# Routing of eight heads in batches, with pair sums only where they can be among the best 16

## The reference, cut to what matters

```python
def block(xb):
    qry = (xb @ wq).reshape(PEER_BLOCK, R_HEADS, 2, HALF_KEY)
    s = jnp.einsum('prsk,snk->prsn', qry, subkeys)
    s1, i1 = lax.top_k(s[:, :, 0], PEER_TOPK)       # 16 of 128
    s2, i2 = lax.top_k(s[:, :, 1], PEER_TOPK)
    cand_s = (s1[..., :, None] + s2[..., None, :]).reshape(..., 256)
    cand_i = (i1[..., :, None] * N_KEYS + i2[..., None, :]).reshape(..., 256)
    top_s, top_pos = lax.top_k(cand_s, PEER_TOPK)   # 16 of 256
    idx = jnp.take_along_axis(cand_i, top_pos, axis=-1)
    gate = jax.nn.softmax(top_s, axis=-1)
    u = jnp.take(u_tab, idx, axis=0)
    act = jax.nn.gelu(jnp.einsum('prkd,pd->prk', u, xb))
    v = jnp.take(v_tab, idx, axis=0)
    return jnp.einsum('prk,prkd->pd', gate * act, v)
```

## Time and profile before

| what | us |
|---|---|
| median of three runs | 6728.52 (6718.85 to 6743.54) |
| the profiled execution | 6727.06 |
| its span, first to last instruction | 6725.2 |
| DVE busy in the span | 4249.0 |
| POOL busy in the span | 3074.3 |
| expert part of the first layer, first dot to last sum | 1867.1 |

### The profile page before, as it was taken

The page is one execution under the profiler, slowest core; times in us unless marked ns, Lnnn a source line. Parts: engine busy times, 40 slices in busy tenths (PEclk is TensorE's granted clock), DMA queues, the critical chain, the costliest instruction groups (busy, mean ns, idle before and its releaser), DMA issues. The chain is left out here.

```text
span 6725.2 us, 54716 instructions
## 1 busy us (share of the span) xinstructions
PE 4633.8 (69%) x17681; PEld 2732.2 (41%) x17681; DVE 4249.0 (63%) x8313; ACT 1205.2 (18%) x2414; POOL 3074.3 (46%) x2828
## 2 busy tenths in 40 slices
PE   7989886998665627170889898869986655362617
PEld 3785555564222202020347855565642222120202
DVE  2551448049788798988325514571597887979783
ACT  2421143010111101010124211430101111010101
POOL 0000012027777777777600000120277777777775
PEclk8999988999887869595979999989998888686959
DMA  4001010659999999999930011006599999999998
GB/s 144 26 0 38 25 38 3 232 206 344 375 344 355 373 412 372 409 377 409 361 114 25 0 39 37 25 21 229 216 340 387 334 376 371 409 369 407 367 413 331
DMA packets 506080, 1623.44 MB, mean 241 GB/s; under 512 B 48148, under 2 KB 60586, under 8 KB 505658
## 3 DMA queue, kind: packets, MB, share of 16 engines
q0 software_dynamic: 368640, 1342.34, 51.7%
q1 hardware_dynamic: 137202, 278.23, 11.4%
HBM read 1601.45 MB, written 21.56 MB: 241 GB/s over the span
## 5 line engine op out<-in xcount | busy, mean ns | idle before, releaser
L1167 PE MATMUL ps<-slab,arena 128*128 128x512 f32 x744 | 356.1, 616 | 674.1 <-DMA slab<-in_peer_v,peer_idxs 670.6
L1167 PE MATMUL ps<-arena 128*128 128x512 f32 x1128 | 528.6, 604 | 84.1 <-DMA arena<-in_peer_v,peer_idxs 70.0
L731 PE MATMUL ps<-hT,slab 128*128 128x512 f32 (+1 forms) x2048 | 568.5, 439 | 6.1 <-DVE arena L1687 6.1
L1167 PE MATMUL ps<-states,arena 128*128 128x512 f32 x792 | 378.9, 620 | 264.4 <-DMA states<-in_peer_v,peer_idxs 230.3
L2273 POOL DMA_INDIRECT arena<-in_peer_u,peer_idxs x400 | 478.1, 1195 | 176.9 <-issue 98.6
L1525 ACT ACTIVATE arena<-consts,arena 128x128 f32<-128x128 f32 x800 | 313.7, 400 | 1264.0 <-PE ps L1167 1259.7
L2120 DVE CUSTOM_DVE_ANT_0 arena<-arena 128x1024 f32<-128x1024 f32 x400 | 494.2, 1242 | 34.0 <-DMA arena<-in_peer_u,peer_idxs 30.5
L1167 PEld LDWEIGHTS ps<-slab,arena 128*128 128x128 f32 x744 | 135.0, 193 | 891.3 <-DMA slab<-in_peer_v,peer_idxs 660.5
L2273 POOL DMA_INDIRECT states<-in_peer_u,peer_idxs x300 | 359.1, 1197 | 266.9 <-PE ps L1123 149.0
L2273 POOL DMA_INDIRECT arena<-in_peer_v,peer_idxs x400 | 420.4, 1051 | 132.7 <-issue 94.0
L1167 PE MATMUL ps<-hT,arena 128*128 128x512 f32 x456 | 219.6, 619 | 375.1 <-DMA hT<-in_peer_v,peer_idxs 371.3
(11 more groups left out here) (323 smaller groups left out, 9370.2 us busy)
## 6 DMA issues: line engine op xcount, KB each, us to landing
slab<-in_w_in SPq DMA_DIRECT2D x50, 2048.0 KB, 7.8
slab<-in_ada_w SPq DMA_DIRECT2D x18, 2048.0 KB, 8.4
arena<-in_w_branch SPq DMA_DIRECT2D x24, 1024.0 KB, 12.2
slab<-in_w_out SPq DMA_DIRECT2D x8, 2048.0 KB, 12.3
arena<-mod_scratch SPq DMA_DIRECT2D x28, 512.0 KB, 9.0
arena<-in_ada_w SPq DMA_DIRECT2D x6, 2048.0 KB, 9.8
slab<-in_peer_wq SPq DMA_DIRECT2D x6, 2048.0 KB, 19.6
x_scratch<-arena SPq DMA_DIRECT2D x16, 512.0 KB, 5.5
```

The source lines that it names most:

```text
L731: last = mm(bank(i0 + c, part), wt[:, k, c * P:(c + 1) * P], hT[:, k, t0:t0 + tn], start=(k == 0), stop=(k == KC - 1))
L1167: last = mm(ps[4 + half][:, :], diag[i % DIAGS], row(e, 1, j)[:, 512 * half:512 * half + 512], start=(i == 0), stop=(j == PE_SLOTS[-1]))
```

## The change

Two things are changed in routing. First, heads are routed in batches: in block 0 heads 0 and 1, then 2 to 4, then 5 to 7; in the other blocks four and four. All that follows the passes over the scores is done for the batch in one operation. Second, the table of pair sums shrinks from 256 to 54 columns. In two falling lists the pair (i, j) cannot be among the best 16 when (i + 1)(j + 1) > 16; five rectangles (`RECTS`) cover what is left. A place in the 54 columns is turned into i and j without shift and mask: the places at which rows i begin (`starts`) are compared with it, and the differences of neighbouring first numbers, summed up to i, give the first key's number; the place minus the row's start gives j.

Part of the diff:

```diff
+RECTS = ((0, 0, 1, 16), (16, 1, 2, 8), (24, 2, 4, 5), (34, 4, 8, 3), (46, 8, 16, 1))
+N_CAND = 54
+BATCH = 4
...
-                cand3 = PK["cand"].rearrange("p (i j) -> p i j", j=TOPK)
...
-                    elif step < 24:
-                        side = (step - 18) // 3
-                        pos, out = (("pi", "e1"), ("pj", "e2"))[side]
-                        if (step - 18) % 3 == 0:
-                            w(dk, "e1" if side else "pj")
-                            dk.mark(tt(cand3, bc_last(PK[pos], TOPK), bc_mid(C["iota"], TOPK), ALU.is_equal), ("eq", side))
-                        elif (step - 18) % 3 == 1:
-                            w(dk, ("eq", side))
-                            dk.mark(tt(cand3, cand3, bc_mid(PK["tif"][:, TOPK * side:TOPK * side + TOPK], TOPK), ALU.mult), ("eqv", side))
-                        else:
-                            w(dk, ("eqv", side))
-                            dk.mark(v.tensor_reduce(PK[out], cand3, AX.X, ALU.add), out)
...
+                def routing(e, first, last, spare):
...
+                    for i in range(nr):
                         if e == 0:
+                            dve.wait_ge(scored, first + i + 1)
+                        for side in (0, 1):
+                            c, o = 256 * (first + i) + P * side, 32 * i + TOPK * side
+                            yield from top16(dk, tv[:, o:o + TOPK], ti[:, o:o + TOPK], PK["sc"][:, c:c + P], (i, side))
...
+                    for c0, i0, i1, n in RECTS:
+                        rows_, shape = i1 - i0, [P, nr, i1 - i0, n]
+                        dk.mark(tt(cand3[:, :, c0:c0 + rows_ * n].rearrange("p r (i j) -> p r i j", j=n),
+                                   tv3[:, :, i0:i1].unsqueeze(3).broadcast_to(shape),
+                                   tv3[:, :, TOPK:TOPK + n].unsqueeze(2).broadcast_to(shape), ALU.add), ("cand", c0))
+                        yield
+                    w(dk, ("cand", RECTS[-1][0]))
+                    for i in range(nr):
+                        o = TOPK * i
+                        yield from top16(dk, fv[:, o:o + TOPK], fp[:, o:o + TOPK], cand[:, N_CAND * i:N_CAND * (i + 1)], ("c", i))
...
+                    dk.mark(tt(tv3[:, :, 1:TOPK], ti3[:, :, 1:TOPK], ti3[:, :, 0:TOPK - 1], ALU.subtract), "d1")
+                    yield
+                    shape = [P, nr, TOPK, TOPK]
+                    reached = PK["sc"][:, 256 * first:256 * last]
...
+                    dk.mark(tt(flat(reached), bc_last(fpf, TOPK), bc_mid(C["starts"], TOPK * nr), ALU.is_ge), "reached")
+                    yield
...
+                    dk.mark(tt(flat(spare), flat(reached), bc_mid(C["dstarts"], TOPK * nr), ALU.mult), "start_parts")
+                    yield
...
+                    dk.mark(v.tensor_reduce(pj, flat(spare), AX.X, ALU.add), "start")
+                    yield
...
+                    dk.mark(tt(four(reached), four(reached), tv3[:, :, 0:TOPK].unsqueeze(2).broadcast_to(shape), ALU.mult), "e1_parts")
+                    yield
...
+                    dve.sem_clear(dk.sem)
+                    dve.sem_inc(routed, nr)
...
-                dots(0, routing(0, 2, R_HEADS), lambda j: 2, (100, 122, 124, 126))
+                def rest_of_first_block():
+                    for first in (2, 5):
+                        yield from routing(0, first, first + 3, ACC_ALL[:, 0:768])
+                dots(0, rest_of_first_block(), lambda j: 3, (100, 122, 124, 126))
```

More of the change, by code:

```diff
@@ L60, in _layout @@
                     ("posq1", P), ("posk0", 1), ("posk1", 1), ("rot", P), ("cos", TS), ("sin", TS),
[L61 removed]
+                    ("iota", TOPK), ("starts", TOPK), ("dstarts", TOPK), ("eps5", 1), ("eps6", 1), ("sel", GROUPS * P)):
         CONST_COLS[name] = (at, n)
@@ L83, in constants @@
     row = lambda v: np.broadcast_to(v, (P, len(v)))
+    starts = np.concatenate([at + n * np.arange(i1 - i0) for at, i0, i1, n in RECTS])
     value = {
@@ L90, in constants @@
         "posk0": P - 1 - j, "posk1": j, "rot": rot, "cos": np.cos(ang), "sin": np.sin(ang),
-        "iota": row(np.arange(TOPK)), "eps5": np.full((P, 1), LN_EPS), "eps6": np.full((P, 1), NORM_EPS),
+        "iota": row(np.arange(TOPK)), "starts": row(starts), "dstarts": row(np.diff(starts, prepend=0)), "eps5": np.full((P, 1), LN_EPS), "eps6": np.full((P, 1), NORM_EPS),
         "sel": (j == np.arange(GROUPS * P)[None, :] // P),
@@ L290, in trunk_program @@
         ex = [Stage(f"ex{e}", csem, plan) for e in range(NB)]
-        route = Stage("route", csem, plan, "dve")
-        STAGES = ([mods1, dnp, dn, dno, rtp, rt, rto, hgp, hg, hgo, mods2] + [st[g] for st in (merge, resid, peq) for g in GRP] + ex
-                  + [route])
+        route_sem = csem("route")
+        route = {n: Marks(route_sem, plan, ("route", n)) for n in (2, 3, 4)}
+        STAGES = ([mods1, dnp, dn, dno, rtp, rt, rto, hgp, hg, hgo, mods2] + [st[g] for st in (merge, resid, peq) for g in GRP] + ex)
         clearable += list(slab_loaded.values()) + bias_loaded + [
@@ L651, in trunk_program @@
         at = 11264
-        for x, n in (("keys", 2 * N_KEYS), ("cand", TOPK * TOPK), ("tv", 2 * TOPK), ("tif", 2 * TOPK), ("fv", TOPK), ("pi", TOPK),
-                     ("pj", TOPK), ("e1", TOPK), ("e2", TOPK), ("gs", R_HEADS), ("fvs", NB * SLOTS), ("dot", SLOTS), ("gel", SLOTS),
+        for x, n in (("keys", 2 * N_KEYS), ("cand", BATCH * N_CAND), ("tv", BATCH * 2 * TOPK), ("tif", BATCH * 2 * TOPK),
+                     ("fpf", BATCH * TOPK), ("pj", BATCH * TOPK), ("e1", BATCH * TOPK), ("e2", BATCH * TOPK), ("gs", R_HEADS), ("fvs", 2 * SLOTS), ("dot", SLOTS), ("gel", SLOTS),
                      ("coef", SLOTS), ("gate", SLOTS)):
@@ L658, in trunk_program @@
         PKU = {}
-        for x, n in (("ti", 2 * TOPK), ("fp", TOPK), ("pu", TOPK), ("idxs", NB * SLOTS)):
+        for x, n in (("ti", BATCH * 2 * TOPK), ("fp", BATCH * TOPK), ("idxs", NB * SLOTS)):
             PKU[x] = sb("peer_" + x, [P, n], U32)
@@ L2059, in _, with top16 @@
-                ROUTE_STEPS = 28
-                def routing(e, first, last):
-                    for r in range(first, last):
-                        if e == 0:
-                            dve.wait_ge(scored, r + 1)
-                        for step in range(ROUTE_STEPS):
-                            route_step(e, r, step)
-                            yield
+                def top16(dk, vals, idx, src, key):
+                    dk.mark(v.max(vals[:, 0:8], src), ("m0", key))
+                    yield
+                    w(dk, ("m0", key))
+                    dk.mark(v.max_index(idx[:, 0:8], vals[:, 0:8], src), ("i0", key))
+                    yield
+                    dk.mark(v.match_replace(src, vals[:, 0:8], src, -3e38), ("r0", key))
+                    yield
+                    w(dk, ("r0", key))
+                    dk.mark(v.max(vals[:, 8:16], src), ("m1", key))
+                    yield
+                    w(dk, ("m1", key))
+                    dk.mark(v.max_index(idx[:, 8:16], vals[:, 8:16], src), ("i1", key))
+                    yield
@@ L2071, in finish, with routing_of_block @@
+                TMPD_ALL = arena[:, 2048:3072]
+                ACC_ALL = arena[:, 7168:9216]
+                def routing_of_block(e):
+                    for first in range(0, R_HEADS, BATCH):
+                        yield from routing(e, first, first + BATCH, TMPD_ALL)
                 def finish(e):
@@ L2137, in sums @@
                         w(ex[e].act, ("sc", 3))
-                        aside = routing(e + 1, 0, R_HEADS)
+                        aside = routing_of_block(e + 1)
                     for j in range(SLOTS):
@@ L2154, in sums @@
                         pass
-                for _ in routing(0, 0, 2):
+                for _ in routing(0, 0, 2, ACC_ALL[:, 0:512]):
                     pass
```

114 lines of the change are left out of this document (55 added, 59 removed).

## The result

The changed kernel takes 6746.17 us (median of 20 runs) beside 6722.18 us for the kernel before in the same job: a ratio of 1.003, interval [1.002, 1.004]. That is 24 us more by the medians, within the range of the prediction, but not the "no change" that was forecast: the interval excludes it. Its profiled execution took 6744.98 us, 17.9 more than that of before.

The account below looks back on a forecast made before the run. It took POOL's issue of one gather per expert row to pace the sums, lengthened by DVE's two-input operations. Four sums at +1.4 us and first dots at -5 gave +0.6 a layer, +1.2 in all: 6728 us, range 6668 to 6778.

Parts of the forecast that it names:

- no change: Whole kernel: 6728 us, between 6695 and 6762, within about 0.5% of the kernel before; chance 0.62.
- Routing per head: DVE's routing: 7.7 us a head in batches of four instead of 10.5, 62 us a block against 84.
- 85 dots remain without routing ... I take 1.60: First block's dots after the 43rd: 1.60 us each, between 1.51 and 1.70; stretch 243 us, -5 us a layer.
- the 252 us that the prediction named as a sign of being wrong: First dots stretch: a length below 236 or above 252 us would show the prediction wrong.
- The low one, 1.51: First block's remaining dots: 1.51 us each, as with full buffers, making the stretch 235 us (-13).
- In the first two blocks with 8 buffers I take the same: Sums of the first two blocks: +1.4 us a stretch, the value taken for the later sums with routing.
- the bounds: Sums stretches with routing: between -4.5 us, if long operations hold nothing, and +6.0, if each costs the longest hold.
- The sum: Whole kernel: 4 x 1.4 - 5 = +0.6 us a layer, +1.2 for two layers.
- The rival of long two-input operations: Batch tails: 1.22 us operations hold gathers, +6.0 us a sums stretch, +3 in first dots; 6781 us, chance 0.16.
- slower: Whole kernel: 6762 us or more, about 0.5% over the kernel before; chance 0.16.
- Start: Before the first dot: heads 0 and 1 come out together some 17 us after 1443.33, hidden behind POOL's first gather.

Follow-up runs that it names:

- half_slabs: The changed kernel, but the twelve weight slabs that the merge loads in the first dots bring only half their rows; 6737.46 us, 1.0023 of the kernel before.
- spread_first: The changed kernel, but in block 0's dots routing comes two steps a dot instead of three from dot 22 on; 6733.48 us, 1.0023 of the kernel before.
- the twins: The changed kernel with three long two-input table operations, or three reductions, of a batch issued three times over; 6824.56 and 6818.72 us, 1.0175 and 1.0157 of the kernel before.

## Why the prediction was wrong, step by step

**Routing per head: right.** 20.5 us less a sums stretch for 22 forecast, the long operations within 0.01 us of the 1.22 taken.

**"85 dots remain without routing ... I take 1.60": the step that failed.** The 43rd dot ended at 98.2 us, for 99 forecast. The other 85 took 154.3 us, 6.2 of them a wait for ACT: 1.74 each (the 1.77 of the expectation for half_slabs is from a cut at 1566.0, before that dot). 85 x 0.14 = 12 us a layer, which with 2 us gained elsewhere turns the 242.4 us of the forecast into 252.5, and -5 into +4.4. Both ends of the step's range were too low, and the stretch lies above the 252 us that the prediction named as a sign of being wrong. The low one, 1.51, was read from 8 dots that ate up full buffers; 80 dots can't be fed at that pace. The step asked how fast DVE is once it is free, where the question was how fast rows arrive: POOL, which from the 49th dot on stood still once, for 2.3 us, needed 1.36 us for a gather, 0.3 between two, and time for its other work.

**"In the first two blocks with 8 buffers I take the same": failed too, by less.** The first sums came to +5.0 and +5.7 us, for +1.4; in spread_first and half_slabs, which have the same order of steps there, they are +1.5 to +4.4. A tail of eight long operations makes DVE free rows late when there are 8 buffers. The second block has 8 buffers too, and its sums went -1.9 and +1.1; why they did not lose against the kernel before is not shown, but in the twins they grew as much as the first. The six other stretches went -1.5 on average, inside the bounds but with the other sign; a gather in the third and fourth sums takes 130.10 / 128 = 1.02 and 129.00 / 129 = 1.00 us, for 1.04 before.

**The sum.** It had 2 x 4 x 1.4 = +11 us for the eight sums and 2 x -5 = -10 for the two first dots, which cancel; they measured +1.9 and +9.8. That the total still lies within the range is in part luck: the dots went the wrong way, and the sums cost less than was feared. The stretches without routing (+15.9 us) and the parts ahead of them (-9.8) stood in no term. Nor are 34 us the least that can be told from no change: with 20 runs of each kernel, 24 us are clear.

**The rival of long two-input operations, the wrong mechanism.** It priced holds by the length of routing's operations. Such holds exist, but twelve more of these operations a stretch lengthen the mean gather from 1.05 to 1.06 us in the first sums, and reductions, which hold none of the 18 gathers above, cost as much. The Trainium skill's page "SBUF — State Buffer", section "SBUF: two separate sides", has a VectorE operation with two SBUF inputs hold the shared port pair as an exclusive lock for its whole instruction, if it starts before a GpSimd operation that reads SBUF, and the other way round. The rows here agree only in part: gathers begun 0.1 us or more into such an operation end some 0.81 us behind it, but of 144 begun in its first 0.09 us 50 took their 0.94 us beside it, as the one at 1784.18 in the weighted sum of 1784.12 to 1785.43, and the 616 dots begun some 0.2 us into a gather took 1.23 us, those beside no gather 1.22. So a result "slower" was right in sign for this rival and wrong in cause; it is the burst that leaves the ring full. The profile before showed POOL waiting for dots in the 8 buffers, and I did not carry that into the sums.

**Start: right.** Heads 0 and 1 were done at 1455.3 us, 17 us after their first instruction, and POOL's first gather was again released by PE.

## What to carry to other kernels

Where a queue of transfers is the pace, work woven into the consumer should be spread by its time and not by its number of steps: the same steps took 1.003 of the time before in one order and 0.990 in another. Where the engine that issues the transfers is busy throughout, as POOL in the tail here, a stretch can't repay what a burst left unmoved, so look at bytes over time, and at that engine's waits, in each part of it. And a pace read while buffers are full is not the pace at which they fill.

## What the hardware showed unexpectedly

Whether a gather is held depends on when it starts within DVE's operation. I grouped all gathers of the changed kernel by their start after a two-input operation of over 1.1 us: begun 0.1 us into it they take 1.97 us in the median, at 0.5 us 1.56, at 0.9 us 1.15, at 1.1 us 0.975 (some 880 of the 2560, the usual case). Where the operation starts after the gather they take 0.94 in the median, all groups alike, 464 gathers. Those that start in its first 0.09 us are mixed: 50 take 0.94, such as the one at 1784.18, and 94 some 1.97. A held gather ends 0.81 us after the operation that was running at its start. This looks as if something both need were wanted only for an instant near the gather's start, which no run here tests by itself.
